# Attention values as one-pass products of high and low halves, with two PSUM banks for the result

## What is computed

```python
p  = rms_norm(x) @ w_in            # one projection, its columns shared out below
A  = gated_delta_net(...)          # 8 heads of 128, chunked delta rule
Bf = forgetting_attention(...)     # 16 heads of 64, sigmoid output gate
y  = sigmoid(gA) * (A @ w_branch_a) + sigmoid(gB) * (Bf @ w_branch_b)
x  = x + y @ w_out
x  = x + swiglu(rms_norm(x))
out = rms_norm(x)
```

```python
sc = einsum(q_i, k) * scale + c_i[:, None] - cum_k[None, :]
sc = where(causal mask, sc, -inf)
p  = softmax(sc)
o  = einsum('bhqk,bkhd->bqhd', p, v)
```

## Time and profile before

| | |
|---|---|
| median of the runs | 1318.05 us |
| the profiled execution | 1314.04 us, its span 1312.3 us |
| TensorE busy with products | 1259.4 us, 96% of the span |
| TensorE loading weights (beside products) | 1055.7 us, 80% |
| VectorE, ScalarE, GpSimd busy | 508.4, 474.0, 466.3 us |
| mean granted TensorE clock | 0.981 of full speed |
| the attention steps, with the ninth | about 530 to 811 us of the span |

### The profile page before, as it was taken

One profiled execution on the slowest core, in us unless ns is written; L12 is line 12 of the kernel. 1 busy time (PEld: TensorE's weight loads), 2 busy tenths in 40 slices (PEclk: granted clock), 3 DMA queues, 4 the chain that ended last, 5 costly groups with the idle time before them and its releaser, 6 DMA issues.

```text
span 1312.3 us, 18270 instructions
## 1 busy us (share of the span) xinstructions
PE 1259.4 (96%) x6573; PEld 1055.7 (80%) x6573; DVE 508.4 (39%) x897; ACT 474.0 (36%) x889; POOL 466.3 (36%) x226
## 2 busy tenths in 40 slices
PE   5999989989899999999999999999999999999997
PEld 4868868879779788788888877788888888888886
DVE  4324443342252432366666664543233333331001
ACT  5344462442534523444444342232332222222112
POOL 5334440230321501333333331444344444443443
PEclk9999989998999998999999999899999999999999
DMA  6223321120211311433322222642233333332231
GB/s 168 80 81 96 96 58 48 57 65 25 74 49 37 93 41 49 121 88 88 85 81 83 86 80 95 201 137 81 81 96 96 96 96 96 96 96 96 96 113 64
DMA packets 169638, 113.69 MB, mean 87 GB/s; under 512 B 6257, under 2 KB 157922, under 8 KB 169586
## 3 DMA queue, kind: packets, MB, share of 16 engines
q1 hardware_dynamic: 163218, 98.26, 25.9%
q10 hardware_dynamic: 6368, 14.72, 3.1%
HBM read 104.54 MB, written 8.42 MB: 86 GB/s over the span
## 4 chain that ended last, share of the span: by engine, by line
PE 41%; issue 17%; POOL 5%; DVE 1%; ACT 0%; POOLq 0%; DVEq 0%; ACTq 0%
PE ps L1196 28%; PE ps L1555 9%; POOL w_lo L509 5%; PE ps L1284 3%; PE ps L1178 1%; PE ps L1491 1%; DVE mixT L1169 0%; DVE tmp L1125 0%; DVE Tm L967 0%; DVE y_hi L839 0%; ACT gin L785 0%; DVE Tm L970 0%; DVE L L965 0%; DVEq L65 0%; DVE E L958 0%
## 5 line engine op out<-in xcount | busy, mean ns | idle before, releaser
L509 POOL TENSOR_TENSOR w_lo<-raw,w_hi 128x1024 fp32r<-128x1024 f32 x170 | 418.6, 2463 | 776.6 <-ACT w_hi L573 776.6
L1196 PE MATMUL ps<-h_hi,w_lo 128*128 128x512 f32 x992 | 407.1, 410 | 0.0
L1196 PE MATMUL ps<-h_hi,w_hi 128*128 128x512 f32 x992 | 390.7, 394 | 2.8 <-ACT gate L652 1.7
L1196 PE MATMUL ps<-h_lo,w_hi 128*128 128x512 f32 x992 | 392.2, 395 | 0.0
L573 ACT ACTIVATE w_hi<-raw 128x1024 fp32r<-128x1024 f32 x170 | 180.3, 1061 | 551.5 <-PE ps L1196 458.4
L1196 PEld LDWEIGHTS ps<-h_lo,w_hi 128*128 128x128 f32 x992 | 186.9, 188 | 38.5 <-issue 1.0
L1196 PEld LDWEIGHTS ps<-h_hi,w_hi 128*128 128x128 f32 x992 | 187.8, 189 | 35.0 <-ACT gate L652 2.1
L1196 PEld LDWEIGHTS ps<-h_hi,w_lo 128*128 128x128 f32 x992 | 188.9, 190 | 31.8 <-issue 1.2
L888 DVE SCALAR_TENSOR_TENSOR tmp<-ps,prm,tmp 128x511 f32<-128x511 f32 (+2 forms) x72 | 53.9, 749 | 92.0 <-ACT tmp L603 86.9
L1134 DVE TENSOR_TENSOR f_lo<-tmp,f_hi 128x512 f32 (+1 forms) x22 | 40.5, 1842 | 33.6 <-ACT f_hi L805 33.6
L683 ACT ACTIVATE Tm<-ps 128x512 f32<-128x512 f32 x40 | 21.7, 594 | 84.6 <-PE ps L1178 84.6
(11 more groups left out here) (233 smaller groups left out, 1672.8 us busy)
## 6 DMA issues: line engine op xcount, KB each, us to landing
raw<-in_w_in SPq DMA_DIRECT2D x80, 512.0 KB, 3.8
raw<-in_w_gate SPq DMA_DIRECT2D x22, 512.0 KB, 3.7
raw<-in_w_up SPq DMA_DIRECT2D x22, 512.0 KB, 3.7
raw<-in_w_down SPq DMA_DIRECT2D x22, 512.0 KB, 3.2
gate_dram<-gate ACTq DMA_DIRECT2D x24, 256.0 KB, 2.0
cumb<-cum_dram ACTq DMA_DIRECT2D x8, 512.0 KB, 3.5
raw<-in_w_branch_a SPq DMA_DIRECT2D x8, 512.0 KB, 4.3
raw<-in_w_branch_b SPq DMA_DIRECT2D x8, 512.0 KB, 3.7
```

What stands on the lines that cost most here:

```text
L509: pool.tensor_tensor(w_lo[:, r % 2, :], raw[:, r, :], w_hi[:, r % 2, :], ALU.subtract)\
L1196: return pe.matmul(ps[:, bank, :], wts[wl][k], acts[xl][:, k, :], start=(n == 0), stop=(n == len(PASSES) - 1))
```

## The change

The transposed probabilities are kept as two float32r tensors, `pT_hi` (written by ScalarE) and `pT_lo` (written by VectorE as the transposed result minus `pT_hi`), and the values as high and low halves that lie side by side (`v2`, high written by ScalarE, low by VectorE). In place of one full float32 product of 64 columns there are two float32r products: `pT_hi` by both halves of the values (128 columns) and `pT_lo` by the high half (64 columns). The result of head 0 lies in bank 6 and that of head 1 in bank 7, each with 128 columns for a query block: the main part and the part of the low values. VectorE scales both parts of both heads (four instructions in place of two) and adds them (two new instructions, `o_nat` plus `o_rest`, both in SBUF). `vT` and `o_rest` now use parts of `gate` and `tmp`, and `pT_lo` lies where `probs` lies.

```diff
-            vT = sb("vT", [P, T])
-            v_nat = sb("v_nat", [P, TT, P])
+            v2 = sb("v2", [P, TT, 2, 2, FD], F32R)
...
-            probs = sb("probs", [P, 2 * NS])
-            probsT = sb("probsT", [P, 2 * NS])
+            with ExitStack() as over:
+                probs = over.enter_context(nc.sbuf_tensor("probs", [P, 2 * NS], F32))
+            pT_lo = sb("pT_lo", [P, 2 * NS], F32R)
+            pT_hi = sb("pT_hi", [P, 2 * NS], F32R)
...
+            o_rest = tmp[:, 0, :].rearrange("p (h b d) -> p h b d", h=2, b=TT)
             efo = gate[:, 0, :]
+            vT = gate[:, 1, :]
```

ScalarE:

```diff
-                    act.activation(vT[:, :], ps[:, 0, :], ACT.Copy).then_inc(v_taken, 1)
+                    act.activation(vT, ps[:, 0, :], ACT.Copy).then_inc(v_taken, 1)
+                if attention:
+                    for t, (h, b) in enumerate(TASKS):
+                        n = (b + 1) * P
+                        act.wait_ge(probs_turned, 8 * i - 8 + t + 1)
+                        act.activation(pT_hi[:, START[t]:START[t] + n], ps[:, 4 + t % 3, 0:n], ACT.Copy)\
+                            .then_inc(probsT_high, 1)
+                if products:
                     high_ahead(q, 1)
...
+                    act.wait_ge(v_back, i + 1)
+                    act.activation(v2[:, :, :, 0, :],
+                                   ps[:, 5, :].rearrange("p (t h d) -> p t h d", t=TT, h=2), ACT.Copy)\
+                        .then_inc(v_high, 1)
                     high_ahead(q, 3)
```

VectorE:

```diff
-                        dve.wait_ge(probs_turned, 8 * i - 8 + t + 1)
+                        dve.wait_ge(probsT_high, 8 * i - 8 + t + 1)
                         n = (b + 1) * P
-                        copy(probsT[:, START[t]:START[t] + n], ps[:, 4 + t % 3, 0:n]).then_inc(probsT_ready, 1)
+                        s = slice(START[t], START[t] + n)
+                        dve.tensor_tensor(pT_lo[:, s], ps[:, 4 + t % 3, 0:n], pT_hi[:, s].bitcast(F32),
+                                          ALU.subtract).then_inc(probsT_ready, 1)
...
                     for h in range(2):
-                        dve.tensor_tensor(
-                            o_nat[:, :, h * FD:(h + 1) * FD],
-                            ps[:, 7, :].rearrange("p (h b d) -> p h b d", h=2, b=TT)[:, h],
-                            rsum[:, h * TT:(h + 1) * TT].unsqueeze(2).broadcast_to([P, TT, FD]),
-                            ALU.mult).then_inc(o_taken, 1)
+                        pv = ps[:, 6 + h, :].rearrange("p (b v d) -> p b v d", b=TT, v=2)
+                        own = o_nat[:, :, h * FD:(h + 1) * FD]
+                        dve.tensor_tensor(own, pv[:, :, 0, :], rsum[:, h * TT:(h + 1) * TT].unsqueeze(2)
+                                          .broadcast_to([P, TT, FD]), ALU.mult).then_inc(o_main, 1)
+                    for h in range(2):
+                        pv = ps[:, 6 + h, :].rearrange("p (b v d) -> p b v d", b=TT, v=2)
+                        dve.tensor_tensor(o_rest[:, h], pv[:, :, 1, :], rsum[:, h * TT:(h + 1) * TT].unsqueeze(2)
+                                          .broadcast_to([P, TT, FD]), ALU.mult).then_inc(o_main, 1)
+                    for h in range(2):
+                        own = o_nat[:, :, h * FD:(h + 1) * FD]
+                        dve.wait_ge(o_main, 4 * i - 1 + h)
+                        dve.tensor_tensor(own, own, o_rest[:, h], ALU.add).then_inc(o_taken, 1)
...
-                    copy(v_nat[:, :, :], ps[:, 5, :].rearrange("p (t n) -> p t n", t=TT)).then_inc(v_ready, 1)
+                    dve.wait_ge(v_high, i + 1)
+                    dve.tensor_tensor(v2[:, :, :, 1, :], ps[:, 5, :].rearrange("p (t h d) -> p t h d", t=TT, h=2),
+                                      v2[:, :, :, 0, :].bitcast(F32), ALU.subtract).then_inc(v_ready, 1)
```

TensorE:

```diff
                         if t == 2:
                             pe.wait_ge(probsT_ready, led(probsT_ready, 8 * a))
+                            pe.wait_ge(o_taken, led(o_taken, 2 * a))
...
                         if t == 0:
+                            pe.wait_ge(probsT_ready, led(probsT_ready, 8 * a + 6))
                             pe.wait_ge(b_mul, led(b_mul, a))
                         for k in range(b + 1):
                             s = START[t] + k * P
-                            last = pe.matmul(ps[:, 7, t * FD:(t + 1) * FD], probsT[:, s:s + P],
-                                             v_nat[:, k, h * FD:(h + 1) * FD], start=(k == 0), stop=(k == b))
+                            pe.matmul(ps[:, 6 + h, b * P:(b + 1) * P], pT_hi[:, s:s + P],
+                                      v2[:, k, h, :, :].rearrange("p v d -> p (v d)"), start=(k == 0), stop=False)
+                            last = pe.matmul(ps[:, 6 + h, b * P:b * P + FD], pT_lo[:, s:s + P],
+                                             v2[:, k, h, 0, :], start=False, stop=(k == b))
```

More of the change, by code:

```diff
@@ L304, in hybrid_block @@
         probs_turned = sem("probs_turned")
+        probsT_high = sem("probsT_high")
         probsT_ready = sem("probsT_ready")
@@ L307, in hybrid_block @@
         pv_done = sem("pv_done")
+        o_main = sem("o_main")
         o_taken = sem("o_taken")
@@ L310, in hybrid_block @@
         v_back = sem("v_back")
+        v_high = sem("v_high")
         v_ready = sem("v_ready")
```

## The result

The changed kernel takes 1332.41 us (median of four runs, 1328.44 to 1337.05) against 1319.26 us for the kernel before, measured beside it: a ratio of 1.0107, 95% interval 1.0086 to 1.0128, so 14 us slower. The forecast was 1331 us. The profiled execution took 1333.13 us, its span 1331.4 us.

A forecast was written before the change was run, and what follows sets the result against it. TensorE, busy 96% of the span, was taken as the bound. Products 0, six steps 9.5, ninth call 2.8 and ScalarE 0.7 gave 13.0 us on 1318.05: 1331 us, range 1318 to 1336.

The forecast's parts named there:

- The products, 0 us: On TensorE, weight loads set the price at 0.112 us a pass; 320 loads before and after, so 0 us.
- The additions are held up by `w_lo`: At a step's end, GpSimd's w_lo holds VectorE's additions; the keys' low halves begin at 713.66 instead of 711.92.
- the two orders named: First addition loses or wins against w_lo; either way the second is held to about the same time.
- `k_ready`, 0.40 us a step: Before score 0, TensorE waits 0.40 us a step because VectorE's keys' low halves are late.
- `b_hi` held up in turn, score 3, 1.18 us a step: The next w_lo holds b_hi on VectorE, delaying the scores; TensorE waits 1.18 us before score 3.
- The ninth call, 2.8 us, with up to 3.5 more by the clock: At the seventh crossing TensorE pays VectorE's whole delay, 2.8 us; a lower clock could add at most 3.5, not summed.
- ScalarE in unit 1, 0.7 us: ScalarE's rounded copy of task 0 behind vT delays transposes 3 by 0.1 us a step, 0.7 us over seven.

The follow-up runs named there:

- the form without the second hold: The change with b_hi and b_lo made from the transposed result in PSUM instead of tmp in SBUF, without the output gate; 1323.60 us, ratio 1.0034.
- its early and its late form: Kernel before plus two VectorE instructions, each with two SBUF operands: early 1319.26 us; late, with two scalings repeated in front, 1333.00 us.

## Why the prediction was right

- **The products, 0 us.** Right in the mechanism, and shown three ways: 4.39 against 4.38 us for 40 passes, half the columns for nothing, and 0.110 us for each load left out.
- **The additions are held up by `w_lo`.** Right in place and size; the keys' low halves came within 0.1 us of the time forecast. Of the two orders named, the first addition won, and as said it did not matter.
- **`k_ready`, 0.40 us a step.** Measured 0.34 by the form without the second hold. Set beside a step of before, large product by large product, TensorE in the changed kernel is 0.3 us late behind score 0 and 1.6 us late behind score 3.
- **`b_hi` held up in turn, score 3, 1.18 us a step.** Measured 1.29. Together 1.63 us a step against 1.58, so 9.8 us for six steps where 9.5 stood.
- **The ninth call, 2.8 us, with up to 3.5 more by the clock.** Right, to a tenth: score 3 starts 6.02 us after the step's last transposes of `o_nat` in place of 3.23, so 2.8 us late. The wait in front of it grew to 2.7 us and the clock fell behind it (granted 0.66 from 800 to 810 us). From score 3 to the next transposes of `o_nat` are 22.6 us in place of 20.8, and these 1.8 us are put down to the clock. They are the cost that the forecast named and left out of its sum. The timeline of PE in the changed kernel:

```profile
802.65 0.79 PE L1431 MATMUL ps<-k,q 128*128 128x512 f32 x1 [2.69 <-DVE nmax L1050]
803.24 0.63 PE L1432 MATMUL ps<-kl,q 128*128 128x512 f32 x1
```

- **ScalarE in unit 1, 0.7 us.** Right where it arises, and wrong in the sum. The weight load of task 3's transposes shows 0.31 us of idle time in front of it in the changed kernel:

```profile
741.45 0.42 PEld L1206 LDWEIGHTS ps<-ident,probs 128*128 128x128 f32 x4 [0.31 <-issue]
```

  What that costs TensorE is best read without the additions. From the transposes of `o_nat` to the large product behind task 3 are 13.48 us before (first two lines) and 13.58 without additions (last two), so the forecast's 0.1 us:

```profile
681.69 0.60 PE L1178 MATMUL ps<-ident,o_nat 128*128 128x128 f32 x4
695.17 0.48 PE L1196 MATMUL ps<-h_hi,w_lo 128*128 128x512 f32 x1
...
688.87 0.60 PE L1202 MATMUL ps<-ident,o_nat 128*128 128x128 f32 x4
702.45 0.48 PE L1220 MATMUL ps<-h_hi,w_lo 128*128 128x512 f32 x1
```

  But the lag melts to some 0.02 us in units 2 and 3 of the same step, so a step is as long as that of before (33.46 and 33.45). Part of it goes in unit 2, where the new products stand, part in unit 3, where none do; why is not shown.

- **What the forecast did not see.** That the clock can fall while the new products stand back to back and TensorE is never idle. In the changed kernel itself the profile shows no such fall at that place (its 40 products took 4.39 us).

The sum, 13.0 us, stands against 14.4 in the profiles' attention stretch and 14 in the runs (11 to 17 by the interval). The terms give the difference: 0.3 more in the six steps, 1.8 for the clock, and the 0.7 of ScalarE that did not arrive. That the sum comes so near is in part luck, since the last two errors partly cancel; the mechanism and the sizes of the two holds are not. The forecast time of 1331 us was counted from 1318.05; beside the changed kernel the one before took 1319.26 us.

## What to carry to other kernels

Before splitting a narrow product into one-pass halves, count weight loads, not columns: here two loads before and two after were no gain, with 64 columns or with 128. Before adding a VectorE instruction that reads two tensors of SBUF, or casts from one, look up in the timeline what GpSimd is doing at that moment: behind a 2.4 us instruction of GpSimd a 0.4 us addition took over 2 us, and the delay pushed the next such instruction into the next one of GpSimd. Keeping one operand in PSUM, or starting 0.7 us earlier, left the step as long as before (33.47 and 33.45 us).

## What the runs showed of the hardware that was not expected

- The granted clock fell to its lower level in the midst of products without a gap, 3.7 and 3.9 us into float32r products of 128 and 64 columns, or of 64 alone, in two of the six profiles that have them back to back there; full float32 products of 64 columns at the same place and pace kept it in all three profiles that have them (the kernel before, its early and its late form). With so few profiles this may be chance.
- The hold is decided by who is first to within hundredths of a microsecond (0.05 and 0.02 us in the rows above), and then costs the loser all that is left of the other's instruction and 0.28 us more, every time: the six steps of 35.09 us lie between 35.04 and 35.12.
